# Delta layer: the squares of channels c and c+64 are added on VectorE between two taps of the next convolution, and each sum of squares takes one product

## The reference

```python
qkv = jax.nn.silu(causal_dwconv(qkv, conv_w))       # 4 taps
q = qkv[..., :A_QK]; k = qkv[..., A_QK:2 * A_QK]    # 8 heads x 128 channels each
q, k = l2_norm(q), l2_norm(k)                       # x * rsqrt(sum(x * x) + EPS), over 128 channels
```

## Time and profile before

| | us |
|---|---|
| median of 3 runs | 2256.54 (2253.07 to 2258.7) |
| profiled execution, its own time | 2256.8 |
| its span, first to last instruction | 2255.1 |

### The profile page before, as it was taken

One profiled execution on the slowest core, in us unless ns is written; L12 is line 12 of the kernel. 1 busy time (PEld: TensorE's weight loads), 2 busy tenths in 40 slices (PEclk: granted clock), 3 DMA queues, 4 the chain that ended last, 5 costly groups with the idle time before them and its releaser, 6 DMA issues. The chain is left out here.

```text
span 2255.1 us, 31331 instructions
## 1 busy us (share of the span) xinstructions
PE 2208.6 (98%) x10952; PEld 1849.2 (82%) x10952; DVE 1458.8 (65%) x2691; ACT 1295.9 (57%) x2605; POOL 399.3 (18%) x672
## 2 busy tenths in 40 slices
PE   7999999999999999999999999999999999999999
PEld 6778888887888888778788888888888888888887
DVE  6766758585767675586855829477492855929451
ACT  5656666565666665555646556464665646556530
POOL 2426162433525160560000000000000000000000
PEclk9999999999999999999999999999999999999999
DMA  4213231322222245586111121121211211121241
GB/s 145 57 45 67 76 82 45 82 48 71 50 69 61 59 103 182 189 259 215 53 42 43 43 57 47 39 57 30 66 38 39 66 46 40 38 64 50 92 178 58
DMA packets 301759, 174.26 MB, mean 77 GB/s; under 512 B 97260, under 2 KB 284036, under 8 KB 301604
## 3 DMA queue, kind: packets, MB, share of 16 engines
q1 hardware_dynamic: 301604, 172.26, 26.7%
HBM read 143.66 MB, written 28.56 MB: 76 GB/s over the span
## 5 line engine op out<-in xcount | busy, mean ns | idle before, releaser
L390 PE MATMUL b_front<-g_h_lo,wa_w_hi 128*128 128x512 f32 x2048 | 822.0, 401 | 0.0
L390 PE MATMUL b_front<-g_h_hi,wa_w_hi 128*128 128x512 f32 x2048 | 816.8, 399 | 3.0 <-PEq L1574 3.0
L390 PE MATMUL b_front<-g_h_hi,wa_w_lo 128*128 128x512 f32 x2048 | 818.6, 400 | 0.0
L390 PEld LDWEIGHTS b_front<-g_h_hi,wa_w_hi 128*128 128x128 f32 x2048 | 386.4, 189 | 79.3 <-issue 3.3
L390 PEld LDWEIGHTS b_front<-g_h_lo,wa_w_hi 128*128 128x128 f32 x2048 | 386.4, 189 | 76.7 <-issue 0.2
L390 PEld LDWEIGHTS b_front<-g_h_hi,wa_w_lo 128*128 128x128 f32 x2048 | 386.3, 189 | 75.8 <-issue 0.5
L1298 DVE SCALAR_TENSOR_TENSOR a_acc<-a_x_raw,a_hw,a_acc 128x512 f32<-128x512 f32 x192 | 156.7, 816 | 6.6
L787 POOL TENSOR_TENSOR a_bt<-a_bd,a_bx 128x112 f32<-128x112 f32 (+29 forms) x248 | 120.5, 486 | 214.1 <-DMA a_bd<-u_tiles 195.3
L2227 ACT ACTIVATE b_acc<-b_front,g_gains 128x512 f32<-128x512 f32 x96 | 66.2, 689 | 157.2 <-PE b_front L390 152.6
L2419 DVE TENSOR_TENSOR wa_w_lo<-wa_raw,wa_w_hi 128x1024 fp32r<-128x1024 f32 x79 | 95.6, 1210 | 89.6 <-ACT wa_w_hi L2173 89.6
L790 POOL TENSOR_TENSOR a_bx<-a_bx,a_bt 128x112 f32<-128x112 f32 (+29 forms) x248 | 128.1, 516 | 19.4
(11 more groups left out here) (361 smaller groups left out, 4123.6 us busy)
## 6 DMA issues: line engine op xcount, KB each, us to landing
wa_raw<-in_b_w_in_dram SPq DMA_DIRECT2D x80, 512.0 KB, 3.9
wa_raw<-in_a_w_in_dram SPq DMA_DIRECT2D x48, 512.0 KB, 4.6
p_w_raw<-in_a_w_out_dram SPq DMA_DIRECT2D x40, 512.0 KB, 4.0
a_out<-a_og SPq DMA_DIRECT2D x64, 128.0 KB, 1.9
a_zx<-inverse_tiles SPq DMA_DIRECT2D x16, 384.0 KB, 4.4
p_a_raw<-a_out SPq DMA_DIRECT2D x40, 128.0 KB, 5.1
u_tiles<-a_u SPq DMA_DIRECT2D x8, 512.0 KB, 3.2
a_bd<-u_tiles SPq DMA_DIRECT2D x32, 128.0 KB, 3.6
```

The lines of the kernel that those rows point to most:

```text
L390: last = pe.matmul(out, w[:, k, :], a[:, k, ks], start=(n == 0), stop=(n == 23))
```

## The change

The two 128-row squares become two 64-row squares: channels 0 to 63 into `sg`, channels 64 to 127 into `sq_up`, which lies on partitions 0 to 63. VectorE adds the two between taps 1 and 2 of the next half's convolution. ScalarE rounds the sum into the lower half of `sq_rows`, and VectorE writes the remainder into its upper half. One product by ones adds the 128 rows.

```diff
-        sq_hi = m_.sb("sq_hi", [P, HALF], F32R)
-        sq_lo = m_.sb("sq_lo", [P, HALF], F32R)
+        sq_rows = m_.sb("sq_rows", [P, HALF], F32R)
+        sq_up = m_.sb("sq_up", [P, HALF])
+        low_rows, up_rows = slice(0, P // 2), slice(P // 2, P)
...
-        early.first = (sq_hi, sq_lo)
+        early.first = (sq_rows[:, 0:OUT_TOKENS], sq_rows[:, OUT_TOKENS:])
...
                             act.wait_ge(act_out, n * HALVES + (q + 1 + 2))
-                            act.activation(sq_hi[:, :], acc[:, q % 2], ACT.Square)
-                            act.activation(sg[:, q % 2], acc[:, q % 2], ACT.Square).then_inc(sq, 1)
+                            act.wait_ge(sq_low, n * 4 + q)
+                            act.activation(sg[low_rows, q % 2], acc[low_rows, q % 2], ACT.Square)
+                            act.activation(sq_up[low_rows, :], acc[up_rows, q % 2], ACT.Square).then_inc(sq, 1)
+                            act.wait_ge(sq, (n * 4 + q) * 3 + 2)
+                            act.wait_ge(nsum, n * 4 + q)
+                            act.activation(sq_rows[low_rows, :], sq_up[low_rows, :], ACT.Copy).then_inc(sq, 1)
...
-                        pe.matmul(turn[:, :], g.ones_r[:, :], sq_hi[:, :], start=True, stop=False)
-                        pe.matmul(turn[:, :], g.ones_r[:, :], sq_lo[:, :], start=False, stop=True).then_inc(nsum, 1)
+                        pe.matmul(turn[:, :], g.ones_r[:, :], sq_rows[:, :], start=True, stop=True).then_inc(nsum, 1)
...
                                     if m is not None and s == CHAIN0 and tap == 2:
                                         merge(m, 0, 1)
+                                    if tap == 2 and 1 <= q < 5:
+                                        dve.wait_ge(sq, (n * 4 + (q - 1)) * 3 + 1)
+                                        dve.tensor_tensor(sq_up[low_rows, :], sq_up[low_rows, :],
+                                                          sg[low_rows, (q - 1) % 2], ALU.add).then_inc(sq, 1)
...
-                            dve.wait_ge(sq, n * 4 + (q + 1))
-                            dve.tensor_tensor(sq_lo[:, :], sg[:, q % 2], sq_hi[:, :].bitcast(F32), ALU.subtract
-                                              ).then_inc(sq_low, 1)
+                            dve.wait_ge(sq, (n * 4 + q) * 3 + 3)
+                            dve.tensor_tensor(sq_rows[up_rows, :], sq_up[low_rows, :],
+                                              sq_rows[low_rows, :].bitcast(F32), ALU.subtract).then_inc(sq_low, 1)
```

## The result

The changed kernel takes 2266.27 us (median of 4 runs, 2264.49 to 2268.21) against 2256.86 beside it: ratio 1.0044, 95% interval 1.0027 to 1.0061, or 9.4 us more. Its profiled execution spans 2265.3 us, against 2255.1.

What follows compares the result with a forecast made beforehand. TensorE, busy 98%, was taken as the bound. Waits of 16.3 us in heads 1 to 7 plus 2.4 in head 0, less 7.4 for removed products, gave +11.3: 2267.8 us, range 2259 to 2276 (likeliest case's own range 2262 to 2275).

Steps and rivals of the forecast that it cites:

- A product is worth 0.23 us: TensorE's queue: 32 products removed, each worth the 0.23 us between starts, 7.4 us less in all.
- `vn` is late in sum 0: Sum 0, heads 1 to 7: ScalarE's rounding waits for VectorE's addition, vn queues behind it; TensorE waits 1.18 us per head.
- The merge of sum 2: Sum 2, heads 1 to 7: VectorE's merge behind the remainder has no margin; it and TensorE come 0.71 us later.
- Sum 1: Heads 1 to 7: bc 0.25 us late, the remainder 0.29; 0.30 taken, as one wait shields the other.
- Sum 3: Heads 1 to 7: remainder 0.60 us later against 0.46 us of margin, leaving a wait of 0.14 us.
- Head 0: Its four sums already wait for VectorE; 0.60 us more each, 2.4 us in all.
- The remainder on the upper rows: VectorE, output on partitions 64 to 127: remainder starts 0.10 us later and lets the next start 0.11 later.
- The sum: Whole kernel: seven heads' waits 16.3 us, plus 2.4 for head 0, less 7.4: +11.3 us, 2267.8 us.
- the sum alone waits: Rival, chance 0.13: ScalarE's queue absorbs the block, vn in time, only VectorE's delay counts; +7.3 us, 2263.8 us.
- all is hidden: Rival, chance 0.07: the addition is hidden and the products come off whole; -7.4 us, 2249.1 us.
- half the waits: Rival, chance 0.06: TensorE may hold more margin than its rows show; +2.0 us, 2258.5 us.
- the block spreads: Rival, chance 0.08: sums 1 and 3 lose as much as sum 0 behind the rounding; 13.4 us more, 2281.2 us.

Runs made afterwards that it cites:

- the run with one product: Kernel before, with the remainder's product left out of the four sums (remainder still computed and waited for); ratio 0.9968.
- Two runs, one on each engine: Changed kernel with ScalarE's rounding moved behind the eviction of vn, ratio 1.0012; changed kernel with VectorE's addition of sum 0 one tap earlier, ratio 1.0010.
- the rounding behind `vn`: Changed kernel with ScalarE's rounding moved from behind the squares to behind the eviction of vn; ratio 1.0012.
- the remainder on the low rows: Changed kernel with the remainder written over sq_up on partitions 0 to 63, upper rows of sq_rows zero, so sums leave it out; ratio 1.0032.
- two more moves of that kind: On top of the rounding behind vn: sum 2's remainder moved behind the next slot's merge, 0.9985; then also sums' product behind the projection, 2248.26 us, 0.9954.

## Why the prediction was right, point by point

The time (2267.8 forecast, 2266.3 measured), the sign and the mechanism held, except at sum 3. By the steps of the prediction:

**A product is worth 0.23 us.** Shown by the run with one product, 7.2 us for 32. The 131 ns of the Trainium skill ("TensorE: Matmul & The Clock Gate", Back-to-back issue gap) would have given an estimated 4.2 us, outside that interval.

**`vn` is late in sum 0.** Forecast 1.18 us per head, measured 1.09 by the starts around it in head 4 (1.53 - 0.44), and 0.10 more because the product that has waited starts the next 0.54 instead of 0.44 us later: from line 1150 to the sum 2.31 us, from line 1146 to the sum before 1.12 (451.62 to 452.74), together 1.19. The chain that was forecast from the addition to `vn`'s end, 3.19 us (450.00 to 453.19), took 3.17 (457.03 to 460.20). Two runs, one on each engine, show the block to be the cause. ScalarE's two squares weren't free, as the prediction had it: they start 0.63 us apart where the two before started 0.52 apart. In sum 0 of head 4 this falls ahead of the 1.86 us of waiting and costs nothing.

**The merge of sum 2.** Forecast 0.71, measured 0.69 in its row (4.8 over 7). It goes when the remainder leaves its front.

**Sum 1.** Forecast 0.30, as the larger of `bc` and the remainder, with the addition inheriting GpSimd's 0.95 us. This holds in two of seven heads (1 and 3); in the other five the addition kept its 0.68 us and the tap behind it paid. More on that below. Between the sums 0 and 1 TensorE's starts drift by -0.03 to +0.31 us in the seven heads, and with the saved 0.23 the waits are 0.20 to 0.54.

**Sum 3.** Forecast 0.14, measured 0.35: the starts of sums 2 and 3 of head 4 lie 10.15 us apart before and 10.27 after, 0.12 more, and with the saved 0.23 that is 0.35. Here two things were wrong, together 0.2 us in each of 7 heads.

First, the remainder's margin. It comes 0.58 us later, as forecast (0.60): it ends 9.64 us behind the start of sum 2 before (475.54 to 485.18) and 10.22 after (484.20 to 494.42). But the product that is gone lay between the two sums, and TensorE comes 0.23 us sooner while VectorE doesn't. The run with one product shows it: the remainder still ends 9.63 us behind the start of sum 2 (474.43 to 484.06), and the next sum starts at 9.93 instead of 10.15. The step "behind each the evictions and merges are released by TensorE's own next products, and they move with it" doesn't hold for this one.

Second, the prediction looked for a late `bc` at sum 1 only. At sum 3 ScalarE's block makes it late as well, in all 7 heads, and 0.32 of the 0.35 us are lost there: the products that read it start 0.22 us later than they would, and the next ones another 0.10. Neither wait adds to the other. With the rounding behind `vn` no product waits for `bc`, and the remainder alone keeps the sums 10.27 us apart; with the remainder on the low rows it is free in time, and `bc` keeps them 10.25 apart.

**Head 0.** Forecast 2.4 us more waiting, measured 2.6 (7.0 less 4.4).

**The remainder on the upper rows** starts later and lets the next start later. Forecast 0.10 and 0.11, measured 0.12 and 0.11 against the run on the low rows. In the rows of layer 1 a semaphore could have done it; here the row that is written makes the difference. The Trainium skill, "VectorE: DVE Perf Modes", section Two Vector instructions with no wait between them, says that an instruction whose output starts in another quadrant (32 partitions) than the last output into the same memory starts only when every earlier one has finished; these rows agree, both for the remainder and for the instruction behind it.

**The sum.** Forecast +11.3, measured +9.4, inside the own range of the likeliest case; the interval of the ratio is +6.1 to +13.8 us, so the time alone can't tell the two apart. Per head the forecast has 2.33 - 0.92 = 1.41 us, and the table above has 1.44. The profiled execution itself is 10.2 us longer, and it isn't a clean ledger: 1.5 us are the clock phase ahead of the change, 2.0 lie behind the last sum of head 7, where the change does nothing, and the idle time of TensorE that the profile puts down to issue fell from 6.5 us (4.1 and 2.4, heads 1 to 7) to 2.7 (1.4 and 1.3). Before, heads 5, 6 and 7 had 1.36 us of it each, ahead of line 999; after, only head 3 had it. From the last sum of head 0 to the first of head 1 the changed kernel takes 61.34 us against 62.90, although `vn` is late in that stretch too. What moves the stalls I didn't test, and what this stretch gained stays open.

Of the rivals, "the sum alone waits" fell with the row of `vn`, "all is hidden" with the time, "half the waits" with the rows of sum 2 and head 0, and "the block spreads" with sums 1 to 3, where `vn`'s reader doesn't wait; a small part of it is true, as `bc` is late at sum 3 by 0.32 us in every head, not by 1.18.

## What to carry to other kernels

On an in-order engine an instruction that waits costs what stands behind it, so before putting a cross-engine round trip (square here, add there, round here) into one slot, look what is queued behind its last step and how much margin its reader has. Putting the waiting instruction behind the urgent one gave back 7.2 of the 9.4 us by the ratios, and half of the loss by the rows of heads 1 to 7, with the same instructions, and two more moves of that kind made the kernel 0.0046 x 2257 = 10.4 us faster than before. And a product taken off a full engine pays only if that engine's next wait isn't for something that another engine makes at its own pace: it then comes sooner, and waits longer. A wait that goes may uncover another at the same place, as at sum 3, so each needs its own margin.

## What the runs showed of the hardware that was not expected

GpSimd's mask and VectorE's addition block each other, and either may lose. In heads 1 and 3 the addition takes 1.80 us at sum 1; in the other five it takes 0.68, GpSimd's instruction 2.51 instead of 1.29, and the taps behind pay: 2.44 us for two, 1.52 elsewhere. VectorE, then GpSimd, in head 4:

```profile
468.23 0.68 DVE L1297 TENSOR_TENSOR a_sq_up<-a_sq_up,a_sg 64x512 f32<-64x512 f32 x1
468.83 2.44 DVE L1306 SCALAR_TENSOR_TENSOR a_acc<-a_x_raw,a_hw,a_acc 128x512 f32<-128x512 f32 x2
```
```profile
468.21 2.51 POOL L756 TENSOR_TENSOR a_um<-a_u,g_level_mask 128x512 f32<-128x512 f32 x1 [12.50 <-PE a_lev L1150]
```

and VectorE in head 1, where GpSimd's instruction starts at 153.65 and takes 1.29:

```profile
153.67 1.80 DVE L1297 TENSOR_TENSOR a_sq_up<-a_sq_up,a_sg 64x512 f32<-64x512 f32 x1
```

In head 4 and in head 1 GpSimd's start is recorded 0.02 us ahead of the addition's, so the recorded starts don't tell who will lose. The Trainium skill, "SBUF — State Buffer", section Summary: rules for kernel authors, says that where a VectorE instruction has two inputs in SBUF, as the addition has, and GpSimd's reads SBUF, the second to issue is blocked until the first finishes. That one of the two is blocked, the rows confirm; which one was the second to issue, they don't resolve. VectorE's queue loses 0.9 to 1.1 us either way, but at sum 1 only a blocked addition hands it on to ScalarE: in two heads TensorE's products wait there for `bc`, 0.5 us in all, in the other five not. It isn't bound to these two heads: with the remainder on the low rows such waits come at sum 1 of heads 1, 3, 6 and 7, with the addition of sum 0 one tap earlier in head 1 alone.
